# Last block of a two-block transformer kernel: another order of the output projection's tiles, another split of the copies, another place for the last top-k rounds

## What is computed

```python
def second_block(x, ...):
    xn = rms_norm_2(x, norm_gain)
    q_a, k_a, v_a, g_a, q_i, k_i, w_i, c_q, c_kv, k_rope, g_b = split(xn @ w_in)
    ...                                   # norms and rope
    # 8 heads A: every query keeps the top 128 keys of an index score
    o_a = indexer_sparse_attention(q_a, k_a, v_a, q_i, k_i, w_i, pos)
    # 8 heads B: block-causal attention, chunks of 64
    o_b = chunk_causal_attention(q_b, k_b, v_b, pos)
    mixed = concat([o_a * silu(g_a), o_b * silu(g_b)])
    return x + mixed @ w_out
```

## Time and profile before

| | |
|---|---|
| median of 3 runs | 1691.25 us (1690.85 to 1691.68) |
| the profiled execution | 1693.96 us, of which its span is 1692.1 us |
| instructions | 23366 |
| busy over the span | PE 98%, weight loads 82%, POOL 42%, ACT 38%, DVE 34% |
| granted TensorE clock over the span | 0.996 |
| attention loop of the last block, with the first tiles of the projection | about 1566 to 1644.5 us |
| rest of the output projection | 1644.5 to 1689 us |

### The profile page before, as it was taken

The page is one execution under the profiler, slowest core; times in us unless marked ns, Lnnn a source line. Parts: engine busy times, 40 slices in busy tenths (PEclk is TensorE's granted clock), DMA queues, the critical chain, the costliest instruction groups (busy, mean ns, idle before and its releaser), DMA issues.

```text
span 1692.1 us, 23366 instructions
## 1 busy us (share of the span) xinstructions
PE 1660.8 (98%) x9334; PEld 1383.2 (82%) x9334; DVE 580.5 (34%) x1159; ACT 648.3 (38%) x957; POOL 707.1 (42%) x554
## 2 busy tenths in 40 slices
PE   6999999999999999999999999999999999999998
PEld 6787889898888888897977898888888887888676
DVE  3459325450000011421247240100001445789651
ACT  4653534452212222522457342222222545553650
POOL 3533233434454455445232434444455433454222
PEclk9999899999999999999999999999999999999999
DMA  5212110413222222232130112222322232222001
GB/s 199 76 52 99 51 51 26 160 63 115 99 97 88 102 97 99 88 114 98 61 115 2 67 62 97 99 99 99 128 100 93 84 123 100 75 75 100 26 1 50
DMA packets 23427, 144.99 MB, mean 86 GB/s; under 512 B 3505, under 2 KB 4273, under 8 KB 7345
## 3 DMA queue, kind: packets, MB, share of 16 engines
q1 hardware_dynamic: 23344, 143.83, 24.1%
HBM read 141.72 MB, written 2.10 MB: 85 GB/s over the span
## 4 chain that ended last, share of the span: by engine, by line
PE 67%; issue 13%; POOL 11%; DVE 5%; ACT 2%; DMA 1%; POOLq 0%; SPq 0%; ACTq 0%; DVEq 0%
POOL wlo L2745 10%; PE PS L452 5%; PE PS L453 5%; PE PS L454 5%; PE PS L485 4%; PE PS L338 4%; PE PS L343 4%; PE PS L487 4%; PE PS L346 4%; PE PS L486 4%; PE PS L961 2%; PE PS L1638 2%; PE PS L466 2%; PE PS L1657 2%; PE PS L467 2%
## 5 line engine op out<-in xcount | busy, mean ns | idle before, releaser
L2745 POOL TENSOR_TENSOR wlo<-wraw,whi 128x512 fp32r<-128x512 f32 (+1 forms) x476 | 628.0, 1351 | 821.2 <-ACT whi L145 821.2
L145 ACT ACTIVATE whi<-wraw 128x2048 fp32r<-128x2048 f32 (+1 forms) x119 | 225.8, 1898 | 237.8 <-PE PS L346 181.4
L452 PE MATMUL PS<-hT_hi,whi 128*128 128x512 f32 x704 | 274.0, 389 | 0.0
L453 PE MATMUL PS<-hT_lo,whi 128*128 128x512 f32 x704 | 273.9, 389 | 0.0
L454 PE MATMUL PS<-hT_hi,wlo 128*128 128x512 f32 x704 | 273.9, 389 | 0.0
L1544 DVE TENSOR_TENSOR act_sb<-sil,PS 128x512 f32 x44 | 30.3, 688 | 428.6 <-ACT sil L1519 428.6
L1519 ACT ACTIVATE sil<-PS 128x512 f32<-128x512 f32 x44 | 26.4, 601 | 355.2 <-PE PS L454 335.3
L452 PEld LDWEIGHTS PS<-hT_hi,whi 128*128 128x128 f32 x704 | 132.2, 188 | 28.1 <-issue 0.6
L454 PEld LDWEIGHTS PS<-hT_hi,wlo 128*128 128x128 f32 x704 | 132.2, 188 | 27.5
L453 PEld LDWEIGHTS PS<-hT_lo,whi 128*128 128x128 f32 x704 | 132.2, 188 | 27.0
L485 PE MATMUL PS<-whi,hT_hi 128*128 128x512 f32 (+2 forms) x288 | 112.6, 391 | 0.1
(11 more groups left out here) (415 smaller groups left out, 3000.8 us busy)
## 6 DMA issues: line engine op xcount, KB each, us to landing
wraw<-wpack SPq DMA_DIRECT2D x125, 1024.0 KB, 4.9
gain<-gains SPq DMA_DIRECT2D x10, 512.0 KB, 6.5
x_sb<-x SPq DMA_DIRECT2D x8, 512.0 KB, 6.7
out<-x_sb SPq DMA_DIRECT2D x3, 512.0 KB, 2.7
csb<-consts SPq DMA_DIRECT2D x1, 704.0 KB, 13.7
out<-x_sb SPq DMA_DIRECT2D x2, 256.0 KB, 2.0
vh<-vecs SPq DMA_DIRECT2D x1, 96.0 KB, 6.3
small<-vecs SPq DMA_DIRECT2D x1, 80.0 KB, 12.1
```

Source lines behind the costliest of these rows:

```text
L145: act.activation((whi[q % 2] if static is not None else hi_of_slot(n))[:, w], wraw[q % 2][:, w], ACT.Copy).then_inc(w_hi, 1)
L452: nc.tensor.matmul(o, whi[q][w], hT_hi[:, k, :], start=(k == 0), stop=False)
L453: nc.tensor.matmul(o, whi[q][w], hT_lo[:, k, :], start=False, stop=False)
L2745: p.tensor_tensor(lo[:, a:b], wraw[q][:, a:b], hi[:, a:b].bitcast(F32), ALU.subtract).then_inc(w_lo, 1)
```

## The change

Nothing but the last block is touched, and every product is still computed once.

1. `pe_last`: after the loop the order becomes slot 1 on tile 2; slot 0 on tile 0; slot 0 on tile 1 (with which slot 0 is used up); slot 1 on tiles 3, 0, 1. Slot 2 on tile 0 now takes the weight pieces one at a time.
2. `copies`: VectorE gets 15 whole copies (macros 0, 1, 4, 6 and 9 to 19) and 4 halves (2, 3, 7, 8), ScalarE 1 whole copy (5) and the other 4 halves.
3. `ahead=True`: in the iterations m < 20 VectorE does `dve_spread` ahead of its copy and not behind it. In the iterations 20 to 22 the order stays.
4. The 8 top-k rounds that were hooked to the iterations 0 to 7 now go with the iterations 0, 1, 2, 3, 4, 6, 8, 9.

```diff
-            def __init__(self, before, macros, copies, lag, banks, turned, outs, p, pt, result, factor):
-                self.macros, self.copies, self.lag = macros, copies, lag
+            def __init__(self, before, macros, copies, lag, banks, turned, outs, p, pt, result, factor, ahead=False):
+                self.macros, self.copies, self.lag, self.ahead = macros, copies, lag, ahead
...
+                    spread = self.ended(m - 1 - self.lag)
+                    if self.ahead and m < self.n:
+                        for g in spread:
+                            self.dve_spread(g)
                     if 0 <= m - 1 < self.n:
                         self.dve_copy(m - 1)
                     for g in self.ended(m - 1):
                         if m < self.n:
                             self.dve_inverse(g)
-                    for g in self.ended(m - 1 - self.lag):
-                        self.dve_spread(g)
+                    if not self.ahead or m >= self.n:
+                        for g in spread:
+                            self.dve_spread(g)
...
-        LAST = Last(FIRST, couple_macros(), 2 * ["a", "av", "a", "a", "av"] + 2 * ["a", "av", "v", "a", "av"], 2, ((4, 5), (6, 7)), (0, 1), (2, 3), ap, apt, gated, gates)
+        LAST = Last(FIRST, couple_macros(), ["v", "v", "av", "av", "v", "a", "v", "av", "av"] + 11 * ["v"], 2,
+                    ((4, 5), (6, 7)), (0, 1), (2, 3), ap, apt, gated, gates, ahead=True)
...
-                if m < 3 or tiles[0]:
+                piece = m > 1 and tiles[0] == 0
+                if not piece:
                     low_ready(t, n)
...
-            slot(1, [2, 3], False)
+            slot(1, [2], False)
             t.wait_ge(sem("at_spread"), LAST.z["spread"] + LAST.slabs)
             slot(0, [0], False)
-            slot(1, [0], False)
             t.wait_ge(sem("at_final"), LAST.z["final"] + LAST.slabs)
             slot(0, [1], True)
-            slot(1, [1], True)
+            slot(1, [3, 0, 1], True)
...
-            LAST.dve(0, {m: lambda: top(1) for m in range(8)})
+            LAST.dve(0, {m: lambda: top(1) for m in (0, 1, 2, 3, 4, 6, 8, 9)})
```

More of the change, by code:

```diff
@@ L2531, in slot @@
                             lambda kk, tt: hT_lo[:, (2 * m + kk + 4) % 8, tt * P:(tt + 1) * P],
-                            lambda tt: t.wait_ge(sem("at_lo"), LAST.z["lo"] + (4 if m < 2 else 8)), tiles, m == 3 and tiles[0] == 0, halves, used)
+                            lambda tt: t.wait_ge(sem("at_lo"), LAST.z["lo"] + (4 if m < 2 else 8)), tiles, piece, halves, used)
             def first_tile(tt, m, spread):
```

## The result

| | before | after |
|---|---|---|
| median | 1691.44 us (4 runs, 1690.85 to 1691.68) | 1680.7 us (4 runs, 1679.74 to 1682.63) |
| profiled execution | 1693.96 us | 1679.74 us |
| its span | 1692.1 us | 1678.0 us |
| its granted clock | 0.996 | 0.997 |

The ratio is 0.9933, with a 95% interval of 0.9921 to 0.9945: under 1%, and clear of no change. The change gains 10.7 us where 9.5 was forecast, and the median lies 1.1 us under the forecast of 1681.8 and 0.1 us under the low end of the range. One later run of the kernel before took 2871.38 us at a granted clock of 0.641 and is left out of every number here.

A forecast was written before the change was run, and what follows sets the result against it. TensorE, busy 98% of the span, was taken as the bound, so only its waits and low-clock stretches could yield time. -6.10 - 1.27 - 2.65 + 0.53 = -9.5 us took the median from 1691.25 to 1681.8 us, range 1680.8 to 1686.

The forecast's parts named there:

- the low end of the range: Best case for the whole kernel: 1681.2 us with the 0.53 us at the end hidden, less 0.4 for spread, 1680.8.
- signs listed for "right": TensorE never idle from slot 1 on, clock 1.00, splits 8.2 us apart, prompt turn, no scores waits, 0.5 us before slot 0.
- Part 1: Output projection's tile order: the 4.53 us late start of slot 2 and 1.57 us of half clock go, 6.1 us gained.
- the last piece of slot 3: Output projection, slot 3 on tile 0: last piece arrives with 0.15 us to spare; priced at 0, bounded by 0.5 us.
- The two terms: At slot 2 on tile 0: 4.53 us of late start, and 1.57 us lost at the half clock behind it.
- Part 2: Attention loop's opening: VectorE copies macro 0, so the turn of macro 1 no longer waits; gain 1.27 us.
- Part 3: Attention loop: gate rows ahead, copies to VectorE; six waits before scores and one turn's wait go, 2.65 us gained.
- hairline margins: A heads' loop: scores released at 3.5 against TensorE's 3.56 us, or 3.67 against 3.72; VectorE 31.3 of 33.2 us, 94%.
- Part 4: End of the loop, iteration 20: macro 19's whole copy precedes the gate rows, delaying slot 0 on tile 3; cost 0.53 us.
- Rival A: A heads' loop: VectorE becomes the bound if its instructions' overlap is lost; 1683.8 us, at worst 1686; chance 0.14.
- Rival B: Output projection: the order brings nothing, slot 2 waits for something other than the buffer; 1687.9 us, chance 0.05.
- Rival C: Loop: VectorE's whole copies take longer than 1.22 us; at 2.31 us each the kernel is slower, 1695.3 us; chance 0.02.

The follow-up runs named there:

- order_only: Kernel before, with only the new order of the tiles and slot 2 by pieces; median 1687.31 us, ratio 0.9969, last part 120.12 us.
- loop_only: Changed kernel with the old order of the tiles and its old waits in the output projection; median 1688.59 us, ratio 0.9975, last part 122.14 us.
- two_behind: Kernel before, with slot 0 used up ahead of two tiles of slot 1 instead of one, slot 2 still waiting for all four pieces; median 1687.97 us, ratio 0.9976.
- pieces_only: Kernel before in its old order of tiles, but slot 2 on tile 0 takes the weight pieces one at a time; median 1688.85 us, ratio 0.9977.
- old_copies: Changed kernel with the old division of copies between ScalarE and VectorE, gate rows still ahead; median 1684.13 us, ratio 0.9956, last part 117.95 us.
- ahead_20: Changed kernel with the gate rows ahead of the copy in iteration 20 too; median 1681.28 us, ratio 0.9931, last part 115.54 us.
- dve_load: Changed kernel with one more unused VectorE operation in each of iterations 10 to 19; median 1683.47 us, ratio 0.9944, last part 117.65 us.
- first_copy_only: Kernel before with one letter changed, macro 0 copied by VectorE; median 1692.2 us, ratio 0.9996, last part 125.67 us.

## Why the prediction came out as it did

**The mechanism was right; the step that failed is the low end of the range.** Of the signs listed for "right", all are in the profile after: no idle time from slot 1 to the end, clock 1.00 throughout, the two splits 8.2 us apart (8.16), the turn right behind the scores in iteration 2, no wait of scores, half a microsecond before slot 0 on tile 3. One reading was off by a little: the fall of the clock was put behind the stall, but it came at 1665.2, 0.3 us before TensorE started again.

**Part 1, the order: -6.10, measured -6.00.** order_only gives 5.81 and shows that what is missing there is the last piece of slot 3, 0.25 where I had 0, inside the bound of 0.5. The prediction let the split of slot 3 start 0.53 us behind slot 2 on TensorE, as it did in order_only, and found a margin of 0.15 there; it had left out the 0.15 us or so from the end of the last piece to the matmul that waits for it, and counted the pieces 0.2 us too early. In the changed kernel the same place shows no gap, because its split started 0.3 us earlier, which the prediction did not foresee: that this term came out at 0 is luck. The two terms behaved as described: a stall of the same length is in loop_only, with 4.28 us for the first tile, and in two_behind and pieces_only, where the stops are short, the clock stays at 1.00.

**Part 2, the opening: -1.27, measured -1.46.** The 0.19 more is the 0.16 us by which ends and starts of TensorE overlap when it doesn't stop: the wait row shows 1.27 idle, and the turn came 3.16 us behind the scores before and 1.73 after, 1.43 apart. For the waits in front of scores I had added 0.065 us each for just that; for this one I had not.

**Part 3, the gate rows and the copies: -2.65, measured -2.91** (0.55 and 2.36). With the B heads it is right to 0.05. With the A heads 0.3 us more came, and it comes from turns: in the two macros with 256-column blocks the scores took 1.23 us before (1606.92 to 1608.15) and take 1.07 now (1600.02 to 1601.09). I had taken the 1.23 for TensorE's own time. It held 0.16 us of waiting for ScalarE's copy (L1696, 1607.08 + 1.02 = 1608.10), too little for the trace to give it as a wait. old_copies brings these back (0.16 and 0.19 us). The hairline margins held: VectorE had 31.33 us of work in the ten iterations, against 31.3 forecast, and at 95% no turn waited for a copy.

**Part 4: +0.53, measured +0.49,** and taken back by ahead_20 (0.51).

**The rivals.** Rival A needed the overlap of VectorE's instructions to be lost. It is not: the copy of the turned macro starts at 1603.29, 0.07 us ahead of the end of the row before it (1602.68 + 0.68). The sentence that the prediction took from the Trainium skill ("VectorE: DVE Perf Modes", The DRAIN you can't avoid), that the next operation waits for an empty pipeline, would have lost the overlap; this trace does not agree with it. The same section adds that a next operation that the engine does not hold starts earlier, and with that the trace agrees. The other place that the prediction cites from it (the same page, Specifications) states only which memory VectorE and ScalarE sit closer to; the price of 0.2 us a copy is from the rows. But the point from which A is true is near: dve_load passed it with 4.5 us of work more in ten iterations, 1.6 us of which TensorE felt. Rival B fell with order_only. Rival C fell with the copies' rows: all fifteen whole copies took between 1.210 and 1.225 us in their new company.

**What failed: the low end of the range,** 1680.8. It was made of two steps, and both were too small.

The first is the best case of the sum. It took the gains of parts 2 and 3 as the most that there could be ("bounds 0 and 2.65") and let only the 0.53 us of part 4 be hidden. Part 4 cost 0.49 us, but parts 2 and 3 brought 1.46 and 2.91 where 1.27 and 2.65 stood, 0.45 us more. With these two the best case is 0.45 us lower, and the range would have held the time.

The second is the 0.4 us taken off "for the runs' spread". That was the distance between the lowest run and the median of three runs of before. The 57 runs of the kernel before that count (four of the first measurement, 53 beside the experiments) have a standard deviation of 1.70 us (1690.78 to 1697.49, median 1692.27), and the 9 of the changed kernel 1.57 us (1679.74 to 1684.28, median 1682.0). A median of three or four such runs can be off by 1 us, and here both were: the shown median of before was 0.8 to 1.2 us under its later ones, and that of after 1.3 us under the pooled one. With 1 us where 0.4 was put, the range would have held the time too.

Of the 1.1 us by which the measured median lies under the forecast, 0.4 is the sum's (9.88 in the last part of the traces against 9.5); the other 0.7 is of the size of this spread. Between the means of all runs the difference is 10.8 us, with a standard error of 0.6.

**What stays open** is the 0.9 us between 9.9 and 10.8. One candidate is seen: the price of the clock behind the old stall was 1.57, 1.56 and 2.49 us in the three traces that have the stall, and a kernel with the old order has that stall, while the changed one has none. If its mean is nearer 2.5 than 1.57, most of the 0.9 is found. The times give it little support: measured by the means of the runs, the ten kernels without that stall gain on average 0.85 us more than their last part says, but loop_only and first_copy_only, which have it, gain 0.46 and 0.48 more as well. Neither these nor three traces can settle it, and the measurement's own error (0.6) covers most of it.

## What to carry to other kernels

When TensorE stands still for a split of weights that is itself waiting for a buffer, count how many tiles of other work stand between the buffer's last use and the wait: each tile put there takes its own length off the stall, and taking the pieces one at a time took 3.4 of 6.1 us off by itself. A copy that holds back the next stage goes ahead of a longer one on the same engine, before work is moved to that engine and not after: with the copy behind, the move that gains 1.9 us costs 2.0. And measure a local change between two instructions of the trace, since whole times carry what the unchanged head of the program does in that run.

## What the runs showed that I had not expected

**The same stop has not the same price.** Three stops of TensorE of 4.37 us, in the same place of the program: the tile behind them took 4.29 (before), 4.28 (loop_only) and 5.21 us (first_copy_only) instead of 2.72. The clock fell to 0.50 some 1.7 us before TensorE started again in the third, and 0.3 us before it did in the first two. The kernels differ, but not in the code of the stop, and each has one trace. Beside a stop of 1.70 us (two_behind), or of 0.79, 0.22, 0.28 and 0.27 within 4 us (pieces_only), the clock stayed at 1.00, and yet TensorE lost 2.0 and 2.7 us, counted as in pieces_only: more than the 1.70 and 1.56 that the rows show as idle.

**The unchanged head of the program varies by over 4 us.** The first matmul of L961 starts at 229.6 us in before, at 225.7 after, and between 225.4 and 229.0 in four others; from there to macro 2's scores it is 1336.3 to 1336.6 us in all of these. The distance between the two traces can be followed from first start to first start of the same line:

- TensorE's first matmul (L266) starts at 11.26 us before and at 10.60 after: 0.66 us.
- By L639 (44.73 and 42.85) it is 1.88. The added 1.22 lie behind the first matmul of the first projection (17.16 and 16.50). Its matmuls of 256 columns start 0.21 us apart while they are slow and 0.12 otherwise. They are slow from 17.5 to 23.3 us before and from 17.5 to 20.8 after. The Trainium skill ("TensorE: Matmul & The Clock Gate", What's actually happening) says that the slow matmuls at a kernel's start vary in number from run to run of one kernel; these rows agree. The clock column doesn't tell here: it reads 1.00 from 17 to 23 us in before, where the matmuls are slow.
- Until L877 (177.08 and 175.10) nearly nothing is added, 1.98.
- By L893 (188.57 and 183.69) it is 4.88, and here the clock column does tell. Stretches of 20 us, before and then after:

```profile
160.00:180.00 20.00, 19.18 (x198) 16.46 (x198) 18.27 (x34) 7.93 (x11) 8.95 (x8) 0.92 0.27 96
180.00:200.00 20.00, 18.14 (x276) 14.94 (x271) 2.25 (x3) 12.95 (x16) 4.97 (x4) 0.82 0.19 65
```

```profile
160.00:180.00 20.00, 19.41 (x220) 16.79 (x221) 16.31 (x31) 10.53 (x14) 6.96 (x6) 1.00 0.31 107
180.00:200.00 20.00, 18.73 (x289) 15.97 (x288) 4.49 (x6) 13.36 (x18) 4.97 (x4) 0.91 0.16 54
```

- From L1144 (211.96 and 206.46, 5.50) to L959 (225.96 and 222.03) 1.57 us are given back; from 200 to 220 us it is after that has the lower clock, 0.91 against 1.00.

So 0.7 us arise before TensorE starts, and the rest where its matmuls run at different speeds in the two executions, in both directions. Why they do is open.
